# The opening of a mixer block: TensorE warms on a tile of ones, and the second weight block goes ahead of the second memory half tile

## The reference

```python
mem_h = rms_norm(mem, mem_norm_g[l])          # mem: 256 x 1024
kv_m = mem_h @ w_mem_kv[l]                    # w_mem_kv: 1024 x 2048
km = rms_norm(kv_m[..., :D_MEM].reshape(B, -1, MEM_HEADS, MEM_HD), mem_k_norm_g[l])
vm = kv_m[..., D_MEM:].reshape(B, -1, MEM_HEADS, MEM_HD)
```

## Time and profile before

| | before |
|---|---|
| median of 3 runs | 976.37 us (976.09 to 976.67) |
| profiled execution | 976.74 us |
| its span | 974.9 us |
| TensorE matmul busy | 970.7 us, 4993 instructions |
| TensorE weight load busy | 857.5 us |
| VectorE busy | 649.9 us |
| ScalarE busy | 518.5 us |
| GpSimd busy | 246.0 us |
| DMA | 103.36 MB, mean 106 GB/s |

### The profile page before, as it was taken

How to read it: one execution, slowest core, us unless ns; L and a number is a source line. 1 busy time by engine, 2 the same in 40 slices (tenths; PEclk the granted TensorE clock), 3 DMA queues, 4 the chain that set the end, 5 groups by cost and what they waited for, 6 DMA issues and landing times.

```text
span 974.9 us, 13868 instructions
## 1 busy us (share of the span) xinstructions
PE 970.7 (100%) x4993; PEld 857.5 (88%) x4993; DVE 649.9 (67%) x1047; ACT 518.5 (53%) x790; POOL 246.0 (25%) x167
## 2 busy tenths in 40 slices
PE   9999999999999999999999999999999999999998
PEld 7888888898989989989898888898998989988887
DVE  6878987779565564653756443796776867735486
ACT  6977644445453453544447211776675857741351
POOL 0100822121011010010110800271622626106600
DMA  8624222112332322332322342707024050638412
GB/s 277 242 87 130 87 87 76 45 54 68 95 97 65 97 65 78 84 95 66 97 87 87 87 129 76 237 12 213 4 80 146 31 153 1 229 94 302 153 43 87
DMA packets 111622, 103.36 MB, mean 106 GB/s; under 512 B 4468, under 2 KB 95192, under 8 KB 111196
## 3 DMA queue, kind: packets, MB, share of 16 engines
q1 hardware_dynamic: 111564, 102.80, 33.5%
q10 hardware_dynamic: 16, 0.00, 0.0%
HBM read 98.59 MB, written 4.20 MB: 105 GB/s over the span
## 4 chain that ended last, share of the span: by engine, by line
PE 100%; POOL 0%; issue 0%; DVE 0%; POOLq 0%
PE proj L619 59%; PE proj L1064 9%; PE att L1091 7%; PE proj L1091 5%; PE att L1141 3%; PE proj L789 2%; PE att L946 2%; PE att L964 2%; PE att L886 1%; PE att L908 1%; PE proj L1021 1%; PE att L954 1%; PE att L935 1%; PE att L679 1%; PE att L1021 1%; PE proj L1141 1%
## 5 line engine op out<-in xcount | busy, mean ns | idle before, releaser
L1807 DVE TENSOR_TENSOR w_lo<-w_raw,w_hi 128x1536 fp32r<-128x1536 f32 (+1 forms) x58 | 124.0, 2138 | 134.8 <-ACT w_hi L1191 129.5
L1191 ACT ACTIVATE w_hi<-w_raw 128x1536 fp32r<-128x1536 f32 (+1 forms) x58 | 97.4, 1680 | 147.9 <-PE proj L619 147.7
L619 PE MATMUL proj<-hT_hi,w_hi 128*128 128x512 f32 x384 | 150.2, 391 | 0.0
L619 PE MATMUL proj<-hT_hi,w_lo 128*128 128x512 f32 x384 | 149.8, 390 | 0.0
L619 PE MATMUL proj<-hT_lo,w_hi 128*128 128x512 f32 x384 | 149.6, 390 | 0.0
L619 PE MATMUL proj<-w_hi,hT_hi 128*128 128x384 f32 (+1 forms) x280 | 96.7, 345 | 0.0
L619 PE MATMUL proj<-w_hi,hT_lo 128*128 128x384 f32 (+1 forms) x280 | 95.3, 340 | 0.0
L619 PE MATMUL proj<-w_lo,hT_hi 128*128 128x384 f32 (+1 forms) x280 | 95.1, 340 | 0.0
L619 PEld LDWEIGHTS proj<-hT_hi,w_lo 128*128 128x128 f32 x384 | 72.1, 188 | 15.2
L619 PEld LDWEIGHTS proj<-hT_lo,w_hi 128*128 128x128 f32 x384 | 72.1, 188 | 14.5
L619 PEld LDWEIGHTS proj<-hT_hi,w_hi 128*128 128x128 f32 x384 | 72.1, 188 | 14.5
(11 more groups left out here) (445 smaller groups left out, 2399.3 us busy)
## 6 DMA issues: line engine op xcount, KB each, us to landing
w_raw<-w_in_in SPq DMA_DIRECT2D x106, 256.0 KB, 3.2
w_raw<-w_in_in SPq DMA_DIRECT2D x32, 512.0 KB, 4.4
w_raw<-w_in_in SPq DMA_DIRECT2D x6, 1024.0 KB, 5.3
w_raw<-w_mem_kv_in SPq DMA_DIRECT2D x10, 512.0 KB, 7.2
yF<-x_in SPq DMA_DIRECT2D x8, 512.0 KB, 7.9
w_raw<-w_branch_in SPq DMA_DIRECT2D x16, 256.0 KB, 3.5
w_raw<-w_branch_in SPq DMA_DIRECT2D x4, 1024.0 KB, 6.4
w_raw<-w_branch_in SPq DMA_DIRECT2D x8, 512.0 KB, 5.5
```

The source lines that it names most:

```text
L619: ins = mm(ps, lhs[a](k, k0), rhs[b](k, k0), start=(first and k == 0 and j == 0), stop=(last and k == KH - 1 and j == 2))
L1191: A_(w_hi[:, kh, :, 0:n], w_raw[:, kh, :, 0:n], ACT.Copy).then_inc(w_hi_done, 1)
L1807: V.tensor_tensor(w_lo[:, kh, :, 0:n], w_raw[:, kh, :, 0:n], w_hi[:, kh, :, 0:n].bitcast(F32), ALU.subtract).then_inc(w_lo_done, 1)
```

## The change

TensorE no longer warms with turns of the identity but with matmuls of a 128x128 tile of ones. The tile is the last eighth of `y_lo`, which is unused at that time, and VectorE sets it in its first instruction. There are 11 of these matmuls before the wait for the identity; after `turn_tile(0)` there are 3 turns of the identity instead of 7, and there is one more behind the first product. SyncE issues piece 1 in front of half tile 1. On TensorE the products of block 1 with memory tile 0 stand in front of `turn_tile(1)`. The three products of block 0 are written out, the low memory part second and the low weight part third. On VectorE the first two blocks of `mem_low(0)` go in front of `piece_low(0)`, and `half_lo` is signalled by the instruction of the second block itself.

```diff
-WARM_TURNS = (8, 7)
+WARM_TURNS = (11, 3, 1)
+        warm_tile = y_lo[:, KT - 1, 0:P]
             load_mem(0)
             load_piece(0, 0, 0)
+            load_piece(1, 0, 0)
             load_mem(1)
-            load_piece(1, 0, 0)
@@ TensorE
+            pe.wait_ge(warm_set, 1)
+            for _ in range(WARM_TURNS[0]):
+                mm(att[3][:, 0:P], warm_tile, warm_tile, start=True, stop=True)
             pe.wait_ge(ident_set, 1)
-            warm(WARM_TURNS[0])
             pe.wait_ge(memg_landed, 16)
...
             pe.wait_ge(w_first_cast, 1)
-            first_products(0, 0, 0, 1, (half_hi, 1), (w_first_lo, 1), (half_lo, 1), weights_last=False)
+            pe.wait_ge(half_hi, 1)
+            mm(banks[0][:, :], memT_hi[:, 0, 0:P], w_hi[:, 0, 0, :], start=True, stop=False)
+            warm(WARM_TURNS[2])
+            pe.wait_ge(half_lo, 1)
+            mm(banks[0][:, :], memT_lo[:, 0, 0:P], w_hi[:, 0, 0, :], start=False, stop=False)
+            pe.wait_ge(w_first_lo, 1)
+            mm(banks[0][:, :], memT_hi[:, 0, 0:P], w_lo[:, 0, 0, :], start=False, stop=False)
+            first_products(0, 0, 1, 2, (w_first_hi, 1), (w_first_lo, 2))
             turn_tile(1)
-            first_products(0, 0, 1, 2, (w_first_hi, 1), (w_first_lo, 2))
             first_products(0, 1, 0, 2, (half_hi, 2), (), (half_lo, 2), weights_last=False)
@@ VectorE
+            V.memset(warm_tile.bitcast(F32), 1.0).then_inc(warm_set, 1)
             V.memset(ones[:, :], 1.0)
...
-            def mem_low(n):
+            def mem_low(n, tiles=range(4)):
...
+                    if n < MT and k == 1:
+                        ins.then_inc(half_lo, 1)
+                if 3 in tiles:
+                    ins.then_inc(xT_lo, 1)
...
             dve.wait_ge(w_first_cast, 1)
+            mem_low(0, (0, 1))
             piece_low(0)
-            mem_low(0)
+            mem_low(0, (2, 3))
             piece_low(1)
             mem_low(1)
```

More of the change, by code:

```diff
@@ L333, in hybrid_block @@
         piece_landed = [None if j in LAST_PIECES else sem(f"piece_landed{j}") for j in range(len(PIECES))]
-        ident_set = sem("ident_set")
+        ident_set, warm_set = sem("ident_set"), sem("warm_set")
         small_landed, vec_landed, ang_landed = sem("small_landed"), sem("vec_landed"), sem("ang_landed")
@@ L1831, in x_scale @@
                                        ALU.mult, ALU.mult).then_inc(x_scaled, 1)
-            def mem_low(n):
+            def mem_low(n, tiles=range(4)):
                 i, half = half_tile(n)
-                if n < MT:
+                if n >= MT:
+                    dve.wait_ge(mem_hi, n + 1)
+                elif 0 in tiles:
                     dve.wait_ge(half_hi, n + 1)
-                else:
-                    dve.wait_ge(mem_hi, n + 1)
-                for k in range(4):
+                for k in tiles:
                     kk = half * 4 + k
                     if n < MT and k == 2:
-                        ins.then_inc(half_lo, 1)
                         dve.wait_ge(mem_hi, n + 1)
@@ L1848, in mem_low @@
                                                  memT_hi[:, kk, i * P:(i + 1) * P].bitcast(F32), ALU.mult, ALU.subtract)
-                ins.then_inc(xT_lo, 1)
+                    if n < MT and k == 1:
+                        ins.then_inc(half_lo, 1)
+                if 3 in tiles:
+                    ins.then_inc(xT_lo, 1)
             def low(n):
```

## The result

The changed kernel takes 978.12 us (median of 20 runs, 976.60 to 980.16); the kernel before 976.58 us (median of 20, 976.08 to 977.39). The ratio is 1.0015, 95% interval 1.001 to 1.0021. So it is slower by 1.5 us, clear of its interval and under 0.2%. What the medians don't say: the kernel before scatters over 1.3 us, the changed one over 3.6. Its fastest run is 0.5 above the fastest of before, its slowest 2.8 above the slowest.

The account below looks back on a forecast made before the run. TensorE was taken to bound the kernel from end to end. To 976.37 us, the median of the kernel before, the second tile's later products added 0.27 and the other terms nothing, giving 976.6; range 975.6 to 977.2.

Parts of the forecast that it names:

- (a): VectorE's memset of the tile of ones takes 0.1 us, costs nothing on the path; TensorE starts near 1.0.
- (b): 11 warming matmuls on TensorE at 0.213 us each take 2.3 us, ending before the first tile's turns at 3.70; cost 0.
- Rival 3: A cold 128-column warming matmul costs as much as a 512-column one, delaying the first tile's turns by 2.0: 978.6, chance 0.03.
- (c): 3 turns for 7 after the first tile: first product 0.7 us earlier, worth nothing on the path.
- (d): Swapped loads exchange landing times: second weight block 6.56, second memory half tile 7.27; later loads unmoved.
- The ends for (e): Earlier weight block leaves a gain of 0.03 to 0.08 us; a second tile landing at 8.5 costs 0.5.
- (e): Second tile's turns queue behind the second block's low half on TensorE; its products start 0.33 us later, 0.27 remaining.
- rival 1: Matmuls of ones lift TensorE's clock before 7.3 us, saving 0.75 where it rose late before: 975.9, chance 0.20.
- Rival 4: TensorE's clock rises late or falls in the new gaps, 10 slow products costing 2 us: 978.6, chance 0.03.
- rival 5: Ones lift the clock no earlier than turns; early part unchanged, sum stands at 976.6, chance 0.10 within the forecast's 0.50.

Follow-up runs that it names:

- e2: Kernel before with 11 matmuls of ones for the 8 turns and 3 turns for 7 after the first tile, old order; 976.65 us, ratio 1.0006.
- e5: Changed kernel with 7 more turns of the identity where TensorE stood idle; 977.94 us, ratio 1.0012.
- e10: Changed kernel, its 11 matmuls of ones replaced by 5 of 512 columns, and 2 of the 3 turns by one such; 977.52 us, ratio 1.0012.
- e3: Changed kernel with the warming of the kernel before (8 and 7 turns, no ones), new order kept; 977.49 us, ratio 1.0011.
- e4: Changed kernel with the second tile's turns put ahead of the second block's low product; 977.18 us, ratio 1.0008.
- e1: Kernel before with 11 matmuls of ones in place of the 8 turns before the identity, 7 turns and old order kept; 976.74 us, ratio 1.0003.
- e11: Changed kernel with 7 turns instead of 3 after the first tile; 977.83 us, ratio 1.0015.
- e8: Changed kernel with only the loads back in their old order, second memory half tile ahead of second weight block; 978.60 us, ratio 1.0019.
- e7: Kernel before with no warming turns at all; 977.40 us, ratio 1.0008.

## Why the prediction was wrong

The forecast was 976.6, range 975.6 to 977.2; measured 978.12.

(a), (b): right. The memset took 0.17, the 11 matmuls started at 1.06 and took 2.61 with the last one's drain, 0.22 apart, and the first tile was turned at 3.80. Rival 3 fell.

(c): the first product came at 5.36 (forecast 5.25), the third at 6.60 (6.45). But "worth on the path: nothing" was the place to doubt. I looked at what the seven turns delayed and not at what they kept up: e2 has no other change of any weight than 3 turns for 7, and gained three runs of eleven that the kernel before never shows.

(d): the block came at 6.32 (6.56) and the tile landed at 7.0 (7.27): right in kind. I held the landings fixed; the profiles put the second block anywhere between 5.5 and 8.0. The ends for (e) have an earlier block and a later tile, but no later block, though (e) had just put it on the path. In e5 and e10 it was taken at 7.70 and 7.20, and with the clock up before the turns these executions took 978.21 and 978.08.

(e): right in mechanism and, with the clock taken out, in size. The fixed terms fit as well: 1.10 more from block to products, and blocks that ScalarE takes on average at 6.6 in the seven profiles with the new loads against 7.3 in the seven with the old ones, leave 0.4 (forecast 0.33 at that place). The lowest runs say 0.3 to 0.6 (976.45 to 976.60 in e3, e4 and the changed kernel against 975.91 to 976.15 in the kernel before and e1).

The step that failed is the one in rival 1 that the sum rests on: "both kernels have the upper level from 8 us on". In the changed kernel's profile the clock rises near 9.0, and three products and most of the turns are cold just where (e) had made them serial. In (e)'s own terms, the last product of the block is on time (8.04, forecast 8.01), the second tile's turns are 0.23 late (8.47 for 8.24), its products 0.47 (9.81 for 9.34), and the low product of the fifth block 0.54 (15.41 for 14.87). So a term put at nothing measured 0.5, in one of the quick executions. I had one execution of the kernel before and took its rise at 7.8 for that of both kernels. That this execution's time still came near the sum (977.20 against 976.74+0.27 = 977.01) is luck: 0.3 came back at 45 us, at the gap that the changed kernel doesn't have. The sum had reckoned that "no wait of TensorE is known that would swallow it".

Rival 4, "the clock rises late", named this cause and got 0.03; rival 1 got 0.20 for the opposite sign, because a page's rule and a row of mine agreed on it. That rule (the Trainium skill, TensorE: Matmul & The Clock Gate, Part 4: PE-mode transpose: turns don't count as TensorE being busy in the way matmuls do) isn't borne out: e3 had only turns behind it and the clock was up at its first product, and e1's matmuls of ones brought the rise to 7.6 where turns had it at 7.8. So rival 5's premise held, and the sum that it was to leave standing fell all the same. The spread of runs in the range, 0.58 from three runs, was too small too: 20 runs of the kernel before cover 1.31.

The rise also moves between executions. TensorE's rows in e3 and in the kernel before are the same within 0.1 us up to the seven turns, and the rise is at 4.7 in one and 7.8 in the other; in e1 and e11 they are the same up to the first product, and it is at 7.6 and 6.2. The same page (Part 1: The HAM clock gate) warns that the moment of the rise varies from run to run; these profiles agree.

What the median is made of can only be estimated, since no profile shows the changed kernel there. With a warm clock the rows give 0.4 over the kernel before, as said. With a clock as late as in e8 they give 3.47 - 1.74 - 0.7 for the second tile's products and 0.4 for the cold products behind, 1.4 in all; measured is 1.5. So a late rise in most executions would explain it, with the order at work in both terms. But late landings under a warm clock reach the same times (e5, e10), and how often each happens stays open. Closing the scatter with more turns (e5, e11) didn't lower the median by more than 0.3, so filling costs about what it saves there, or the late landings of these sessions hid the gain. Medians of different sessions don't settle 0.3 us.

## What to carry to other kernels

An operation that is ready should not be queued behind a wait for a later chain, even if the loads have been put in that order: moving the block ahead of the tile made landing, split, turn and copy one chain, 2.84 us from block to products where it had been 1.74. Before an opening's warming work is shortened, look at the range of twenty runs and not only at one profile: what it holds may be the tail. And one profile gives one sample of a clock rise and of a landing; if a sum needs either, its range must hold the other samples.

## What the runs showed of the hardware

- The granted clock column says 1.00 in all fourteen profiles, also where 512-column products start 0.42 apart. The level must be read from the starts.
- Nearly the same work on TensorE (8 turns, the turn of the gains and 4 turns, from 1.54 us on) was followed by a clock rise at 4.7 us in one execution (e3) and at 7.8 in another (the kernel before).
- A short matmul of ones and a turn cost the same when cold, 0.22 and 0.21 us apart.
- A 256 KB weight block issued at 1.66 us in seven profiles landed 3.8 (e4) to 6.0 us (e5) later. Over all fourteen, with its issue between 1.66 and 2.87, it landed between 5.5 (e4) and 8.0 us (e7) from the start.
